# Input projection of a hybrid encoder step: 512-column strips over six weight slots, a 48-token tile with both halves in one stationary operand, and later sums in the second norm

## What is computed

```python
xn = rmsnorm(h, norm1_g)
z = jnp.einsum('btd,de->bte', xn, w_in)       # 8200 columns: rq rk rv rg fq fk fv ff ga gb
fq = rmsnorm(fq.reshape(b, t, FOX_HEADS, FOX_DIM), q_norm_g)
fk = rmsnorm(fk.reshape(b, t, FOX_HEADS, FOX_DIM), k_norm_g)
logf = jax.nn.log_sigmoid(ff + b_forget)
...                                           # retention and forgetting attention
m = sigmoid(ga) * (ret_o @ w_ret_out) + sigmoid(gb) * (fox_o @ w_fox_out)
h = h + m @ w_o
u = relu(rmsnorm(h, norm2_g) @ w_ff1)
return h + (u * u) @ w_ff2
```

## Time and profile before

| | us |
|---|---|
| median of 3 runs (2205.48 to 2206.36) | 2206.3 |
| the profiled execution's own time | 2208.06 |
| its span in the trace | 2206.4 |
| PE busy | 2159.9 (98%) |
| VectorE busy | 1075.4 (49%) |
| ScalarE busy | 547.0 (25%) |

### The profile page before, as it was taken

The page is one execution under the profiler, slowest core; times in us unless marked ns, Lnnn a source line. Parts: engine busy times, 40 slices in busy tenths (PEclk is TensorE's granted clock), DMA queues, the critical chain, the costliest instruction groups (busy, mean ns, idle before and its releaser), DMA issues.

```text
span 2206.4 us, 35785 instructions
## 1 busy us (share of the span) xinstructions
PE 2159.9 (98%) x14451; PEld 2095.5 (95%) x14451; DVE 1075.4 (49%) x2269; ACT 547.0 (25%) x1110; POOL 65.2 (3%) x116
## 2 busy tenths in 40 slices
PE   6999999999999999999999999989999999999998
PEld 6999999999888999989989999989999999999998
DVE  5444422246666666665565635474333333333333
ACT  4433200012222222231133323231212212122130
POOL 0000000000000000000000000000000000000000
PEclk9999999999999999999999999999999999999999
DMA  3322232423324432336435442111111111111111
GB/s 130 92 80 79 82 105 89 126 87 103 109 78 123 123 103 92 110 108 220 145 121 167 147 159 70 30 39 58 39 48 48 48 48 39 48 48 48 48 39 79
DMA packets 195035, 196.17 MB, mean 89 GB/s; under 512 B 9864, under 2 KB 173640, under 8 KB 194896
## 3 DMA queue, kind: packets, MB, share of 16 engines
q1 hardware_dynamic: 182096, 149.37, 22.5%
q0 software_dynamic: 12800, 44.72, 5.6%
HBM read 145.02 MB, written 49.04 MB: 88 GB/s over the span
## 4 chain that ended last, share of the span: by engine, by line
PE 93%; DVE 4%; issue 1%; ACT 1%; DMA 0%; SPq 0%; DVEq 0%; ACTq 0%
PE ps_mlp L281 36%; PE ps_dense L281 24%; PE ps_dense L297 18%; PE ps_out L901 4%; PE ps_scores L870 2%; PE ps_turn L854 2%; PE ps_scores L946 1%; PE ps_turn L847 1%; PE ps_scores L952 1%; PE ps_scores L951 1%; DVE w_lo L268 1%; DVE act_lo L336 0%; PE ps_turn L852 0%; PE ps_turn L322 0%; PE ps_turn L983 0%
## 5 line engine op out<-in xcount | busy, mean ns | idle before, releaser
L281 PE MATMUL ps_dense<-act_hi,w_lo 128*128 128x352 f32 (+2 forms) x1176 | 392.4, 334 | 0.5 <-DVE gated L1595 0.5
L281 PE MATMUL ps_dense<-act_hi,w_hi 128*128 128x352 f32 (+2 forms) x1176 | 391.6, 333 | 0.0
L281 PE MATMUL ps_dense<-act_lo,w_hi 128*128 128x352 f32 (+2 forms) x1176 | 391.2, 333 | 0.0
L297 PE MATMUL ps_dense<-w_lo,act_hi 128*128 128x256 f32 x1152 | 327.9, 285 | 0.7 <-DVE strip_rows L1377 0.7
L297 PE MATMUL ps_dense<-w_hi,act_lo 128*128 128x256 f32 x1152 | 327.2, 284 | 0.0
L297 PE MATMUL ps_dense<-w_hi,act_hi 128*128 128x256 f32 x1152 | 327.1, 284 | 0.0
L281 PE MATMUL ps_mlp<-act_hi,w_lo 128*128 128x352 f32 x960 | 311.0, 324 | 0.0
L281 PE MATMUL ps_mlp<-act_lo,w_hi 128*128 128x352 f32 x960 | 310.9, 324 | 0.0
L263 ACT CAST w_hi<-w_raw 128x1024 fp32r<-128x1024 f32 x153 | 157.5, 1042 | 617.2 <-PE ps_mlp L281 281.3
L281 PE MATMUL ps_mlp<-act_hi,w_hi 128*128 128x352 f32 x960 | 310.2, 323 | 0.0
L281 PE MATMUL ps_mlp<-u_hi,w_lo 128*128 128x352 f32 x768 | 248.0, 323 | 0.0
(11 more groups left out here) (209 smaller groups left out, 3000.2 us busy)
## 6 DMA issues: line engine op xcount, KB each, us to landing
w_raw<-in_w_in SPq DMA_DIRECT2D x65, 512.0 KB, 4.9
w_raw<-in_w_ff SPq DMA_DIRECT2D x64, 512.0 KB, 3.9
gates<-stage POOLq DMA_DIRECT2D x24, 528.0 KB, 3.4
stage<-gates SPq DMA_DIRECT2D x16, 528.0 KB, 3.7
out<-strip_rows POOLq DMA_DIRECT2D x8, 1024.0 KB, 5.4
negc_rows<-neg_cumsum SPq DMA_DIRECT2D x8, 792.0 KB, 6.6
rotated<-stage POOLq DMA_DIRECT2D x8, 536.0 KB, 3.0
fox_out_T<-fox_stage POOLq DMA_DIRECT2D x8, 528.0 KB, 4.9
```

Of the source, the lines that this page charges most:

```text
L281: mm = nc.tensor.matmul(bank(n)[:, 0:w], lhs[:, k, m0:m0 + P], rhs[:, k, c:c + w], start=(x == 0), stop=(x == 3 * kc - 1))
L297: mm = nc.tensor.matmul(pd[:, n.mod(NB), 0:256], lhs[:, k, t], rhs, start=(k == 0 and q == 0), stop=(k == KC - 1 and q == 2))
```

## The change

**Strips.** There are 8 strips of 512 columns, each of four weight units (two k-chunks a unit); a row tile of a strip is 8 by 3 matmuls of 512 columns into a whole PSUM bank. In the strip stage the weights use six slots (two more, `wxh` and `wxl`): the next strip's units 0 and 1 are cast early in a strip, and units 2 and 3 only when the last row tile is done with units 0 and 1, which it tells by a new count `w_free` (`split_hi_early`). VectorE makes their low halves just before it reads that last tile. **Last tile.** A new operand `xq` holds the 48 tokens' high halves in columns 0 to 63 and their low halves in columns 64 to 127, so that the tile takes 8 by 2 matmuls; VectorE copies one half of the result and adds the other. **Start.** Strip 0's four units are split in VectorE's list behind the first, second and third row tile; squares of row tiles 6 to 8 come later on ScalarE. **Second norm.** `sum_third(1)` moves from `w_o` step 20 to step 22, `sum_third(2)` from the first to the second step of the MLP, and `h_scale` and `h_norm` move with them: `h_norm(1)` and `h_scale(2)` now stand before the first MLP read on VectorE and ScalarE. Loops that ran on registers in the strip stage are written out, and a wait for the store of the second last strip stands before the heads on ScalarE and VectorE.

```diff
+    wxh, _, cosT, sinT, rows0, wxl, gq, gk, crow, lfr, _, lfc, cst, junk, lf, _, rows1, xq = arena([
+        ("w_hi_more", [P, 2, UNIT], F32R), ("stage_end", [P, 96], F32), ("cos", [P, TALL], F32), ("sin", [P, TALL], F32),
+        ("rows_even", [P, NQ, 512], F32), ("w_lo_more", [P, 2, UNIT], F32R), ("gq_bc", [P, P], F32), ("gk_bc", [P, P], F32),
...
-    STRIPS = 16
-    U_FF, N_FF = 2, NQ
+    STRIPS = 8
+    U_FF, N_FF = 4, NQ
...
     def ring(u):
 
-        return 1 + (u.first - U_TURN) % 3 if U_TURN <= u.first < U_GB else u.mod(4)
+        if u.first < U_TURN:
+            return (0, 2, 3, 1, 4, 5)[u.first % 6]
+        return 1 + (u.first - U_TURN) % 3 if u.first < U_GB else u.mod(4)
...
+    def split_hi_early(act, u, uses):
+
+        act.wait_ge(w_in_s[u.mod(2)], u.first // 2 * 16 + 16)
+        act.wait_ge(w_free, uses)
+        nc.scalar.copy(slot_hi(ring(u)), raw[:, u.mod(2), :]).then_inc(w_hi_s, 1)
...
-    def strip_step(pe, n, u, i):
-
-        wait(pe, bank_free, (n - 1).v)
+    def strip_step(pe, s, i):
+
+        n = At(strip_n(s) + i)
+        wait(pe, bank_free, n.first - 1)
+        out = pd[:, n.mod(NB), :]
         for k in range(KC):
-            us = (u + k // 4).mod(4)
-            a, b = (x[:, us, 256 * (k % 4):256 * (k % 4) + 256] for x in (wh, wl))
+            u = strip_unit(s, k // 2)
+            if i == 0 and k % 2 == 0:
+                pe.wait_ge(w_lo_s, u.first + 1)
+            a, b = (x(ring(u))[:, 512 * (k % 2):512 * (k % 2) + 512] for x in (slot_hi, slot_lo))
             t = slice(i * P, i * P + P)
-            for q, (lhs, rhs) in enumerate(((xh, b), (xl, a), (xh, a))):
-                mm = nc.tensor.matmul(pd[:, n.mod(NB), 0:256], lhs[:, k, t], rhs,
-                                      start=(k == 0 and q == 0), stop=(k == KC - 1 and q == 2))
+            pairs = ((xq[:, k, :], b), (xq[:, k, :], a)) if i == NT else ((xh[:, k, t], b), (xl[:, k, t], a), (xh[:, k, t], a))
+            for q, (lhs, rhs) in enumerate(pairs):
+                mm = nc.tensor.matmul(out, lhs, rhs, start=(k == 0 and q == 0), stop=(k == KC - 1 and q == len(pairs) - 1))
+            if i == NT and k in (1, 3, 5):
+                mm.then_inc(w_free, 1)
         mm.then_inc(mm_done, 1)
...
-            if i in (16, 20):
-                sum_third((i - 16) // 4)
+            if i in (16, 22):
+                sum_third((i - 16) // 6)
...
-                if i == 0 and part == 1:
+                if i == 1 and part == 1:
                     sum_third(2)
...
+        def strip_read(s, i):
+            n = strip_n(s) + i
+            dve.wait_ge(mm_done, n + 1)
+            z, r = pd[:, n % NB, :], rows[s % 2]
+            if i < NT:
+                nc.vector.tensor_copy(r[:, i, :], z).then_inc(bank_free, 1)
+                return
+            link(dve, nc.vector.tensor_copy(r[0:LAST, i, :], z[64:64 + LAST]), ch)
+            nc.vector.tensor_tensor(r[0:LAST, i, :], r[0:LAST, i, :], z[0:LAST], ALU.add).then_inc(bank_free, 1)
...
             for i in range(NQ):
-                if i == 0:
-                    wait(dve, stored, s.times(ST_STRIP, -ST_STRIP) if s.i is not None or s.first > 1 else 0)
-                strip_read(s, n, i)
-                if i in (4, 5):
-                    split_lo(dve, u + (i - 2))
+                if i == 0 and s > 1:
+                    dve.wait_ge(stored, ST_STRIP * (s - 1))
+                if i == NQ - 1:
+                    if s + 1 < STRIPS:
+                        for j in (2, 3):
+                            split_lo(dve, strip_unit(s + 1, j))
+                    else:
+                        split_lo(dve, At(U_TURN + 1))
+                strip_read(s, i)
+                if i in (5, 6):
+                    if s + 1 < STRIPS:
+                        split_lo(dve, strip_unit(s + 1, i - 5))
...
+        for q in range(2):
+            split_lo(dve, At(U_MLP + q + 2))
+        h_norm(1, range(KC))
+        h_scale(2)
         for s, (q, j) in enumerate(UP_FIRST):
-            if s < 2:
-                split_lo(dve, At(U_MLP + s + 2))
             up(At(N_MLP + s), q, *O3[j], s, s + 1)
-            if s == 1:
-                h_scale(2)
-            if s in (2, 3):
-                h_norm(2, range(4 * s - 8, 4 * s - 4))
+            if s in (1, 2):
+                h_norm(2, range(4 * s - 4, 4 * s))
```

More of the change, by code:

```diff
@@ L275, in turned_piece @@
         width = UNIT // kc
-        a, b = (x[:, us, :].rearrange("p (k m) -> p k m", m=width) for x in (wh, wl))
+        a, b = (x.rearrange("p (k m) -> p k m", m=width) for x in (slot_hi(us), slot_lo(us)))
         each = 3 * kc // parts
@@ L1112, in root1, with head_squares @@
             nc.scalar.activation(stat[:, 2, 3 * b:3 * b + 3], stat[:, 1, 3 * b:3 * b + 3], ACT.Sqrt).then_inc(a_root, 1)
+        def head_squares(s, tiles):
+            for i in tiles:
+                m = P if i < NT else LAST
+                act.wait_ge(bank_free, strip_n(s) + i + 1)
+                wait(act, sq_s, NQ * s + i - 1)
+                for e in range(4):
+                    ins = nc.scalar.activation(junk[0:m, i % 2, e, :], rows[s % 2][0:m, i, e * P:e * P + P], ACT.Square,
+                                               accum_out=stat[0:m, 0, 4 * i + e:4 * i + e + 1])
+                ins.then_inc(sq_s, 1)
+        act.wait_ge(pad_ok, 1)
         for i in range(3):
@@ L1119, in _ @@
         turn_rows_act(act, 0, (0, 0))
+        for j in range(2):
+            split_hi(act, At(j), At(0))
         square1(4)
@@ L1456, in _ @@
                 ins.then_inc(few_ok, 1)
-        c0 = ch[0]
-        with dve.Fori(0, 2) as i:
-            ch[0] = At(c0.first, 10, i)
-            for s in range(2):
-                strip(At(5 + s, 2, i), gk, 1.0)
-            assert ch[0].first == c0.first + 10
-        ch[0] = At(c0.first + 20)
-        strip(At(9))
-        with dve.Fori(0, 3) as i:
-            for s in range(2):
-                strip(At(10 + s, 2, i))
         def maxes(h, j):
@@ L1635, in ret_head @@
             split(4)
[L1636 removed]
+            dve.wait_ge(a_root, r.times(1, 8))
             root_end(dve, NQ, 1.0, ch)
```

276 lines of the change are left out of this document (143 added, 133 removed).

## The result

The changed kernel takes 2190.73 us (median of 4 runs, 2189.27 to 2192.57) beside 2206.33 us (2205.48 to 2208.41) of the kernel before: a ratio of 0.9928, 95% interval 0.9915 to 0.994. It is 15.6 us faster. The forecast was 33 us, 2173, with a range from 2157 to 2186: the time lies outside it, on the slow side. The profiled execution has a span of 2190.9 us (2206.4 before), and 2192.57 us in all.

The account below looks back on a forecast made before the run. The prediction took PE's work to bound the kernel (93% of the chain that ended last). Its terms, -40.3 + 3.8 + 2.1 + 6.5 - 5.3, summed to -33.2 us, from 2206.3 to 2173 us, range 2157 to 2186.

Parts of the forecast that it names:

- Part A: Strips' matmul stream: 1664 matmuls of 512 columns at 225 ns replace 3456 at 120 ns, -40.3 us.
- I take 213.3 + 11.7 = 225 ns: Strips' 512-column step: 213.3 ns for the columns at 2.4 GHz plus a nearly fixed extra of 11.7 ns.
- Rival 2: Strips: the extra per matmul grows with the width, 240 ns a step, 25 us more, 2198 us; chance 0.06.
- Rival 1: Strips: the extra goes when a matmul lasts longer than 213 ns; 215.7 ns a step, about 2158 us; chance 0.15.
- Part B: Kernel start: weight splits delay the first strip matmul from 29.07 to about 34.6; net +3.8 us, bounds +1 to +6.
- 1.7 us of small waits: Strips 0 and 1: longer strip tiles cover VectorE's work, removing 0.8 us and about 0.9 us of waits.
- Part C: Log gates after strip 1 (ending at T): splits last until T+1.0, PE resumes at T+5.7, not T+3.7; +2.1 us.
- Part D: First head: larger last store lands at T+14.9 (T: strips' end), delaying the score product; +6.5 us, bounds +2 to +9.
- Part E: Second norm: later sums remove two PE waits, waits of 0.7 and 3.5 us come in; -5.3 us, bounds -9 to +1.
- Rival 3: Side terms worse than worked out: Part D at 9, Part E at nothing, some at the start; about 2182 us; chance 0.14.
- Rival 4: Seven strip changes: second-half weights come late, making it slower than before; about 2211 us with 13 us loads; chance 0.03.
- the D and E case: Rival 3's case, Part D at its 9 and Part E at nothing: 2180 to 2188 us, chance 0.14.

Follow-up runs that it names:

- e2_old_layout: Changed kernel with activation rows back at 1152 columns and a 448-byte gap behind the statistics: 2175.47 us, ratio 0.9864.
- m1_steps: Not the reference's computation: streams of 96 matmuls without waits, varying width, offset, row length or neighbour; 226.7 ns a step at 512 columns with aligned operands.
- e8: Changed kernel with activation rows of 1152 columns but without the gap behind the statistics: 2181.03 us, ratio 0.9878.
- e10: Changed kernel with its rows of 1072 columns kept and a 192-byte gap added behind the statistics: 2185.7 us, ratio 0.9904.
- e3: Kernel before the change with a 576-byte gap behind the statistics, rows and strips untouched: 2207.61 us in a single run.
- e1_after_again: The changed kernel run once more, unaltered, beside the kernel before: 2191.75 us, ratio 0.9932.
- e9: e6_split_store with VectorE's two weight splits at strip 1's end moved behind the log gates' last instruction: 2170.0 us, ratio 0.9832.
- e6_split_store: e2_old_layout with the last strip's rows stored in two parts, the first five row tiles early: 2169.42 us, ratio 0.9831.
- e5_old_norm2: e2_old_layout with the second norm's old order, sums after steps 16 and 20 and in the first MLP step: 2180.07 us, ratio 0.9883.

## Why the prediction was wrong, step by step

**Part A, the stream: the direction and 29 of the 40 us.** The failed step is the sentence "I take 213.3 + 11.7 = 225 ns". The result was right within 1.7 ns for the layout from which the extra was read: 226.7 in e2_old_layout, 226.7 in the stream, which is the unshaved 13.3 of 256 columns. That the extra comes back at 512 was in part luck, since at 448 it is 20 ns. What failed is the unspoken step that the extra is a function of the width alone, so that it could be carried from the old rows to rows of 1072. 231.6 instead of 225 ns on 1664 matmuls is 11.0 us: 8.2 from the places of the operands, 2.8 from the 1.7 ns. Rival 2 had the step too high (240 ns) and for another reason, and nothing in m1_steps bears out a proportional extra. Rival 1, that the extra goes above 213 ns, is out: no 512-column stream ran below 226.6. With it falls, for this case, the page's warm rule of N/2.4 + 2.5 ns (TensorE: Matmul & The Clock Gate in the Trainium skill, section "Wait — 56ns, not 53.3ns?"): it gives an estimate of some 216 ns for 512 columns, against 226.7 measured with the best places.

**The MLP, put at nothing: wrong by 6.2 us.** This is the second failed step. The prediction had no term for the MLP and gave no reason. The shorter activation rows and the larger `stat` don't occur in it; they moved the operands of 5184 matmuls. e8, e10 and e3 divide it: 2.7 us by the shared area, 3.4 us by the rows.

**Part B, the start: right.** First strip matmul forecast at 34.6, measured at 34.45, with the third split done at 25.9 for 25.8 and row tile 3 scaled at 28.6 for 28.5. That it fits to 0.15 us is luck: the same kernel started at 33.16 in e1_after_again, where the third unit's cast ended 1.3 us sooner, and the others at 32.8 to 34.1. The 1.7 us of small waits in strips 0 and 1 can't be told apart within the 401 us of the strips; e2_old_layout's strips, 36.4 us shorter than before where 39.9 were forecast and 2.8 of that is the 1.7 ns, leave 0.7 us for all that and for the clock behind the log gates.

**Part C: right in its own number, and e9 shows its limit.** Strip 1 ended one step after the start at 147.92, at 148.15, and PE resumed at 153.95: 5.8 us, 5.7 forecast. The reason given, that the two splits stand in the way until T+1.0, is what e9 confirmed; the surprise was that removing them gains nothing. The clock had 0.1 us in the forecast and cost more: 0.66 over 150 to 160 us against 0.83 over ten us before. PE worked 5.1 us at half speed (152.96 to about 158.1) where it had worked 3.4; that is about 0.8 us, an estimate.

**Part D: right within 1.3 us, wrong in its parts.** The stretch that holds it grew by 6.4 us, 6.5 forecast; but e2_old_layout and e6_split_store put D itself at 5.2 (512.72 less 507.47), the rest of the 6.4 is for the most part the slower pace of its projections (161.7 ns a step in the heads, 160.7 in e2_old_layout). The wait before the score product was 4.7 us, not 6 to 7. The second MB cost less than the 3.2 us taken for it; GpSimd saw the store landed 8.1 us after its issue, against 6.4 for 1 MB:

```profile
457.87 0.52 POOL L768 DMA_DIRECT2D rv_rows_sample<-rows_odd  x1 [8.14 <-DMA rv_rows<-rows_odd]
```

The score product came 15.5 us after the last strip matmul's start instead of 12.1, 3.4 us later. The half clock behind the longer stop made the rest of the 5.2, 1.8 us for 1 to 1.5 forecast. The recorded sum has a slip here besides: T+14.9 and 2.8 us are T+17.7, not T+17.5.

**Part E: right.** 5.3 us forecast, 5.4 between the two kernels, 4.3 to 6.3 by e5_old_norm2. Both waits of the earlier trace rows went, no product with `ones` waits, and the one new wait is 3.4 us for 3.5 forecast. A wait of 0.7 us ahead of the second third isn't in the list of waits.

**The chances.** Rival 3 (2182) had the right neighbourhood by the wrong path, since D and E held. Rival 4 didn't happen at all. The range ended at 2186, the top of the D and E case. It had no room for a mechanism outside the list of parts, and this one cost 16 us with PE's waits near their forecasts.

## What to carry to other kernels

When a kernel is bound by TensorE and a change alters a buffer's row length or moves a base, compare the count of matmuls in the same 100 us of a stage that the change doesn't touch: if it moved (630 to 624 here), look at the operands' addresses within 256 bytes before anything else. Pad rows to a multiple of 256 bytes and keep stationary and moving operands at one place within 256 bytes for 512-column products; for narrower ones measure a few distances, since a gap of 192 bytes gained 8 us in two runs and 17 in two others of the kernel before. Predict such an edit by rows of the same width *and* the same layout; where the layout changes, the bound has to reach to the dearest pace of the width.

## What the runs showed of the hardware that was not expected

- The pace of a stream of fp32r matmuls, each with a weight load of its own, depends on where its two operands stand within 256 bytes: 226.7 to 233.4 ns at 512 columns, where the distance between them decides, 113.4 to 120.0 at 256, 158.3 to 166.8 at 352.
- It depends on what ran before: the same 256-column stream at 113.4 and 117.8 ns, kept for 144 matmuls; one operand in 24 out of place slowed eight steps in a row and made a 512-column tile 228.6 a step instead of 226.7.
- The extra over the columns is no smooth function of the width: 13.3 ns at 256 to 384 and at 512, 20 at 448, and 504 columns cost what 512 do.
- Work of VectorE, ScalarE and the DMA beside the stream cost it nothing that can be seen.
- After a stop of 3.5 or 4.3 us the clock rose again at nearly the same moment (154.7 and 154.3), though PE had started again 0.95 us apart. A stop of 2.2 us was followed by the half clock in the profile of the kernel before and not in that of e3_before_shifted.
